# One hybrid decoder layer: splits four units ahead, the bias row's product inside the first unit, and operations moved between engines

## The reference

```
h = rmsnorm(x, pre_mix_norm);  rq, rk, rv, rg, mq, mk, mv = split(h @ w_in)
ret  = silu(rg) * head_rmsnorm(retention(rotary(rq), rotary(rk) / 8, rv))
moba = softmax(mq @ mk.T / 8 + bias_t[:, bucket(i - j)], causal) @ mv
x = x + rmsnorm(concat(ret, moba) @ w_out, post_mix_norm)
h = rmsnorm(x, pre_ffn_norm)
x = x + rmsnorm((silu(h @ w_gate) * (h @ w_up)) @ w_down, post_ffn_norm)
```

## Time and profile before

| | |
|---|---|
| median of 3 runs | 316.87 us (316.57 to 318.9) |
| the profiled execution's own time | 318.91 us |
| its span, first to last instruction | 317.1 us |
| TensorE busy | 305.3 us, 96% of the span |
| VectorE, ScalarE, GpSimd busy | 182.7, 153.3, 27.6 us |
| granted TensorE clock | 0.998 of full speed |

### The profile page before, as it was taken

How to read it: one execution, slowest core, us unless ns; L and a number is a source line. 1 busy time by engine, 2 the same in 40 slices (tenths; PEclk the granted TensorE clock), 3 DMA queues, 4 the chain that set the end, 5 groups by cost and what they waited for, 6 DMA issues and landing times.

```text
span 317.1 us, 4124 instructions
## 1 busy us (share of the span) xinstructions
PE 305.3 (96%) x1432; PEld 248.8 (78%) x1432; DVE 182.7 (58%) x255; ACT 153.3 (48%) x254; POOL 27.6 (9%) x31
## 2 busy tenths in 40 slices
PE   7999987999999999999999999999999999999992
PEld 3788866888888888768888888888888888888881
DVE  2858265697467487899555555544444454551426
ACT  4889626446608174676444444444433333340322
POOL 4021056000002000540000000000000000000001
PEclk9999999999999999999999999999999999999999
DMA  6999974314541543169965555555566565400003
GB/s 216 398 407 373 413 308 134 134 66 153 180 144 57 198 156 111 66 231 317 367 203 179 179 190 180 168 184 191 198 198 198 198 196 183 149 0 0 0 2 132
DMA packets 17517, 58.35 MB, mean 184 GB/s; under 512 B 1997, under 2 KB 2517, under 8 KB 17504
## 3 DMA queue, kind: packets, MB, share of 16 engines
q1 hardware_dynamic: 17136, 57.06, 51.6%
q0 software_dynamic: 368, 1.11, 1.0%
HBM read 57.10 MB, written 1.06 MB: 183 GB/s over the span
## 4 chain that ended last, share of the span: by engine, by line
PE 85%; DVE 7%; ACT 3%; DMA 2%; POOL 2%; issue 1%; SPq 0%; DVEq 0%
PE bank L951 25%; PE bank L953 24%; PE bank L952 24%; PE bank L961 4%; DVE w_lo L681 2%; DMA raw<-in_w_in 2%; PE bank L978 1%; POOL xs L437 1%; PE bank L982 1%; PE bank L986 1%; ACT w_hi L451 1%; DVE d_lo L876 1%; ACT kz L518 1%; PE bank L1049 1%; DVE res L942 1%
## 5 line engine op out<-in xcount | busy, mean ns | idle before, releaser
L951 PE MATMUL bank<-w_hi,a_hi 128*128 128x512 f32 x256 | 101.9, 398 | 0.0
L953 PE MATMUL bank<-w_hi,a_lo 128*128 128x512 f32 x256 | 100.1, 391 | 0.0
L952 PE MATMUL bank<-w_lo,a_hi 128*128 128x512 f32 x256 | 99.6, 389 | 0.0
L617 ACT ACTIVATE sil<-bank,rstd 128x256 f32<-128x256 f32 x22 | 10.4, 473 | 96.1 <-PE bank L953 93.7
L953 PEld LDWEIGHTS bank<-w_hi,a_lo 128*128 128x128 f32 x256 | 48.0, 188 | 10.6
L952 PEld LDWEIGHTS bank<-w_lo,a_hi 128*128 128x128 f32 x256 | 48.2, 188 | 9.8
L951 PEld LDWEIGHTS bank<-w_hi,a_hi 128*128 128x128 f32 x256 | 48.1, 188 | 9.4
L869 DVE TENSOR_TENSOR w_lo<-raw,w_hi 128x1024 fp32r<-128x1024 f32 x40 | 49.6, 1276 | 6.7 <-ACT w_hi L602 6.7
L681 DVE TENSOR_TENSOR w_lo<-raw,w_hi 128x1024 fp32r<-128x1024 f32 x32 | 42.2, 1345 | 19.4 <-ACT w_hi L451 19.4
L884 DVE SCALAR_TENSOR_TENSOR hid<-bank,rstd,sil 128x256 f32<-128x256 f32 x22 | 10.7, 485 | 73.9 <-ACT sil L617 73.9
L602 ACT ACTIVATE w_hi<-raw 128x1024 fp32r<-128x1024 f32 x40 | 40.5, 1057 | 0.5 <-DMA raw<-in_w_gu 0.5
(11 more groups left out here) (119 smaller groups left out, 307.5 us busy)
## 6 DMA issues: line engine op xcount, KB each, us to landing
raw<-in_w_gu SPq DMA_DIRECT2D x44, 512.0 KB, 4.3
raw<-in_w_dn SPq DMA_DIRECT2D x22, 512.0 KB, 4.6
raw<-in_w_in SPq DMA_DIRECT2D x20, 512.0 KB, 8.5
raw<-in_w_out SPq DMA_DIRECT2D x8, 512.0 KB, 3.2
raw<-in_w_in SPq DMA_DIRECT2D x8, 256.0 KB, 5.8
xs<-in_x SPq DMA_DIRECT2D x2, 512.0 KB, 8.6
bias<-bias_row POOLq DMA_DIRECT2D x1, 1024.0 KB, 10.2
out<-res SPq DMA_DIRECT2D x4, 256.0 KB, 2.0
```

The lines of the kernel that those rows point to most:

```text
L617: act.activation(sil[:, t, :], pg[:, t, 0:FG], ACT.Silu, scale=rstd[:, X1_, t:t + 1]).then_inc(sil_ready[t], 1)
L951: pe.matmul(acc, hi, wh, start=first, stop=False)
L952: pe.matmul(acc, hi, wl, start=False, stop=False)
L953: return pe.matmul(acc, lo, wh, start=False, stop=last)
```

## The change

- `LEAD` is 4: in slot u unit u + 4 is split. The order before the loop loses unit 4, which comes in slot 0.
- The bias row's product stands between the two halves of unit 0; its two tables are issued from ScalarE's queue, ahead of everything there.
- `gp` and `gm` are loaded behind units 8 and 9, not 16 and 18. VectorE, not GpSimd, makes `xg` in slots 7 and 8 and `gp = gm * gp` in slot 9, each behind its lo.
- The copies of k into `kz` are shared: ScalarE the even heads, VectorE the odd ones, at the head of its slot 10.
- `rows_out` for q, k and v stands ahead of hi in slots 4, 8 and 12.
- `xs += mix` stays on GpSimd for tile 0 and goes to VectorE for tile 1, behind lo_gu(1, 1 to 3).
- In the feed-forward part group 1 accumulates in `bank45` and group 0 is turned into `bank01`, so that gate_up(1, 0) need not wait for the first hidden tiles; these are turned in the middle of gate_up(1, 1). In every group both gate_up come first, then down(g - 1, 0), both turns, down(g - 1, 1); ScalarE's and VectorE's orders follow.

```diff
-LEAD = 5
-LO_UNITS = {16: [], 17: [21], 18: [22], 19: [23, 24]}
+LEAD = 4
+LO_UNITS = {16: [], 17: [20], 18: [21], 19: [22, 23]}
...
+G0 = 7
...
-        pg = bank01
-        pt = bank45
+
+        def pg(g):
+            return bank45 if isinstance(g, int) and g == 1 else bank01
+
+        def pt(g):
+            return bank01 if isinstance(g, int) and g == 0 else bank45
...
-                if n == 16:
+                if n == 8:
                     sp.dma_start(gp[:, :], g_pre_ffn.broadcast_to([P, D])).then_inc(gp_loaded, 16)
-                if n == 18:
+                if n == 9:
                     sp.dma_start(gm[:, :], g_post_mix.broadcast_to([P, D])).then_inc(gm_loaded, 16)
...
-            pool.dma_start(rel[0:BUCKETS, :], rel_bias).then_inc(rel_loaded, 16)
-            pool.dma_start(bucket[:, :], bucket_c).then_inc(rel_loaded, 16)
...
-            pool.wait_ge(gp_loaded, 16)
-            pool.wait_ge(gm_loaded, 16)
-            for t in range(NT):
-                pool.wait_ge(x_loaded[t], 16)
-                pool.tensor_tensor(xg[:, t, :], xs[:, t, :], gp[:, :], ALU.mult).then_inc(xg_ready, 1)
-            pool.wait_ge(xg_ready, NT)
-            pool.tensor_tensor(gp[:, :], gm[:, :], gp[:, :], ALU.mult).then_inc(xg_ready, 1)
             pool.wait_ge(k_turned, NT)
-            pool.wait_ge(xg_ready, NT + 1)
+            pool.wait_ge(rstd_ready, NT)
...
+            for c in range(2):
+                cols = slice(c * CW, (c + 1) * CW)
+                pool.wait_ge(mixn_ready, c + 1)
+                pool.tensor_tensor(xs[:, 0, cols], xs[:, 0, cols], mix[:, 0, cols], ALU.add
+                                   ).then_inc(x1_ready[0], 1)
             for t in range(NT):
-                for c in range(2):
-                    cols = slice(c * CW, (c + 1) * CW)
-                    pool.wait_ge(mixn_ready, 2 * t + c + 1)
-                    pool.tensor_tensor(xs[:, t, cols], xs[:, t, cols], mix[:, t, cols], ALU.add
-                                       ).then_inc(x1_ready, 1)
                 factor(FACTORS.index((X1_, t)))
...
+            act.dma_start(bucket[:, :], bucket_c).then_inc(rel_loaded, 16)
+            act.dma_start(rel[0:BUCKETS, :], rel_bias).then_inc(rel_loaded, 16)
...
-            hi_in(4)
...
                 if u == K_T + 1:
                     for t in range(NT):
                         act.wait_ge(k_turned, t + 1)
-                        for odd in range(2):
-                            rows = slice(64 * odd, 64 * odd + 64)
-                            act.activation(kz[rows, odd:MH:2, t * P:(t + 1) * P],
-                                           wk[rows, t, :].rearrange("p (b i) -> p b i", i=P), ACT.Copy
-                                           ).then_inc(kT_ready, 1)
+                        act.activation(kz[0:64, 0:MH:2, t * P:(t + 1) * P],
+                                       wk[0:64, t, :].rearrange("p (b i) -> p b i", i=P), ACT.Copy
+                                       ).then_inc(kT_ready, 1)
+                if u == UPG:
+                    act.wait_ge(nq_ready, 1)
+                    wait_factor(act, X_, NT - 1)
+                    rows_out(qn, 0, lambda t: nq[:, t:t + 1], q_nat)
+                if u == 2 * UPG:
+                    rows_out(kn, 1, r_x, k_nat)
+                if u == 3 * UPG:
+                    rows_out(v, 2, r_x, v_nat)
                 hi_in(u + LEAD)
...
             def group(g, g0, more=True):
 
+                if g0 > 1:
+                    h_hi_part(g - 1, 1)
                 if more:
                     for s in range(GU - 1):
                         hi_gu(g + 1, s, g0 + 1)
                 silu(g, 0)
-                h_hi_part(g - 1, 1)
+                if g0 == 1:
+                    for t in range(NT):
+                        h_hi_part(0, t)
                 if more:
                     hi_gu(g + 1, GU - 1, g0 + 1)
+                silu(g, 1)
                 for j in range(DN):
                     hi_dn(g, j, g0)
-                silu(g, 1)
                 h_hi_part(g, 0)
...
+            hi_gu(1, 3, 1)
             wait_factor(act, X1_, 0)
             silu(0, 0)
-            hi_gu(1, 3, 1)
             x1_squares(1)
-            hi_dn(0, 0, 0)
             wait_factor(act, X1_, 1)
             silu(0, 1)
-            h_hi_part(0, 0)
-            hi_dn(0, 1, 0)
+            for j in range(DN):
+                hi_dn(0, j, 0)
...
             for u in range(N_IN):
+                if u == K_T + 1:
+                    for t in range(NT):
+                        dve.wait_ge(k_turned, t + 1)
+                        dve.tensor_copy(kz[64:P, 1:MH:2, t * P:(t + 1) * P],
+                                        wk[64:P, t, :].rearrange("p (b i) -> p b i", i=P)
+                                        ).then_inc(kT_odd, 1)
...
+                if 0 <= u - G0 < NT:
+                    t = u - G0
+                    dve.wait_ge(gp_loaded, 16)
+                    dve.wait_ge(x_loaded[t], 16)
+                    dve.tensor_tensor(xg[:, t, :], xs[:, t, :], gp[:, :], ALU.mult).then_inc(xg_ready, 1)
+                if u == G0 + NT:
+                    dve.wait_ge(gm_loaded, 16)
+                    dve.wait_ge(xg_ready, NT)
+                    dve.tensor_tensor(gp[:, :], gm[:, :], gp[:, :], ALU.mult).then_inc(xg_ready, 1)
...
             def group(g, g0, more=True):
+                if g0 > 1:
+                    h_lo_part(g - 1, 1)
                 if more:
                     for s in range(GU - 1):
                         lo_gu(g + 1, s, g0 + 1)
                 hidden(g, 0)
-                h_lo_part(g - 1, 1)
+                if g0 == 1:
+                    for t in range(NT):
+                        h_lo_part(0, t)
                 if more:
                     lo_gu(g + 1, GU - 1, g0 + 1)
+                hidden(g, 1)
                 for j in range(DN):
                     lo_dn(g, j, g0)
-                hidden(g, 1)
                 h_lo_part(g, 0)
...
             factor(X1_, 0, 10)
-            lo_gu(1, 1, 1)
+            for s in range(1, GU):
+                lo_gu(1, s, 1)
+            dve.wait_ge(mixn_ready, 2 * NT)
+            for c in range(2):
+                cols = slice(c * CW, (c + 1) * CW)
+                dve.tensor_tensor(xs[:, 1, cols], xs[:, 1, cols], mix[:, 1, cols], ALU.add
+                                  ).then_inc(x1_ready[1], 1)
             hidden(0, 0)
-            lo_gu(1, 2, 1)
-            lo_gu(1, 3, 1)
             factor(X1_, 1, 12)
-            lo_dn(0, 0, 0)
             hidden(0, 1)
-            h_lo_part(0, 0)
-            lo_dn(0, 1, 0)
+            for j in range(DN):
+                lo_dn(0, j, 0)
             group(1, 1)
...
+            def bias_row_product():
+
+                pe.wait_ge(rel_one, 1)
+                pe.wait_ge(rel_loaded, 32)
+                pe.matmul(wk[0:MH, 0, 0:REV], rel[:, :], bucket[:, :], start=True, stop=True
+                          ).then_inc(brow_done, 1)
+
...
+                    if k == 0:
+                        bias_row_product()
...
-                if not (isinstance(g, int) and g == 0):
+                if not (isinstance(g, int) and g <= 1):
                     pe.wait_ge(hid_ready[t], g)
...
+            def first_hidden(s):
+                if s == 1:
+                    for t in range(NT):
+                        turn_hidden(0, t)
+
             def group(g, g0):
-                gate_up(g, 0, g0)
-                turn_hidden(g - 1, 1)
+                for t in range(NT):
+                    gate_up(g, t, g0, hook=first_hidden if g0 == 1 and t == 1 else None)
                 down(g - 1, 0, g0 - 1)
-                gate_up(g, 1, g0)
-                turn_hidden(g, 0)
+                for t in range(NT):
+                    turn_hidden(g, t)
                 down(g - 1, 1, g0 - 1)
...
             gate_up(0, 0, 0, hook=scaled_hook)
             gate_up(0, 1, 0)
-            turn_hidden(0, 0)
             group(1, 1)
             with pe.Fori(2, NF - 2, 2) as g:
                 group(g, 2)
                 group(g + 1, 3)
             group(NF - 1, NF - 1)
-            turn_hidden(NF - 1, 1)
             down(NF - 1, 0, NF - 1, last=True)
             down(NF - 1, 1, NF - 1, last=True)
```

More of the change, by code:

```diff
@@ L237, in hybrid_layer @@
         mixn_ready = sem("mixn_ready")
-        x1_ready = sem("x1_ready")
+        x1_ready = [sem(f"x1_ready{t}") for t in range(NT)]
         gu_done = sem("gu_done")
@@ L529, in _ @@
                         squares(X_, u, c, xs[:, u, c * CW:(c + 1) * CW])
-                if u == UPG:
-                    act.wait_ge(nq_ready, 1)
-                    wait_factor(act, X_, NT - 1)
-                    rows_out(qn, 0, lambda t: nq[:, t:t + 1], q_nat)
-                if u == 2 * UPG:
-                    rows_out(kn, 1, r_x, k_nat)
-                if u == 3 * UPG:
-                    rows_out(v, 2, r_x, v_nat)
                 if u == RQK_T + 1:
@@ L883, in hidden @@
```

(17 more changed lines are left out.)

15 lines of the change are left out of this document (5 added, 10 removed).

## The result

The changed kernel takes 318.91 us (median of 20 executions, 316.61 to 320.86), the kernel before 316.86 us (20 executions, 316.11 to 321.17). The ratio is 1.0046 (95% interval 1.0025 to 1.0066): **slower by 0.5%**, where 314.5 us was forecast. It lies above the range (317.0).

The account below looks back on a forecast made before the run. TensorE, busy 96% of the span, was taken as the bound. Start and input phase 2.8 less feed-forward 0.4 gave 2.4 us, so 314.5 us against the median 316.87; range 311.5 to 317.0, own range 313.3 to 315.9.

Parts of the forecast that it names:

- its own time, then how it stands to the median: Final sum: 2.4 us off the profiled 318.91 gives 316.5; against the median of three runs, 316.87, it gives 314.5.
- the ends of part 3: Start and input phase gain: 4.0 us if copies are in time, about 1 if unit 12 lands 1.8 later.
- part 3: Input phase: lock waits of 1.6 and 2.2 us go; unit 12 lands about 32.2, new 0.85 us wait before head 0.
- part 5: First feed-forward groups: 1.2 us wait goes, down(0, 0) waits 2.1 us; a loss of 0.4 us in all.
- Why the scores wait: Input phase: GpSimd's operation locks VectorE out, so two lo take 3.17 and 3.23 us instead of 1.22.
- The rule on memsets: Shared port: GpSimd's memsets do not lock VectorE and cost nothing; if they did, the sum would give 315.5.
- Part 1, the start: Bias row's product moved into a 1.43 us TensorE stall: gain 0.45 us, bounds a gain of 0.7 and loss of 0.5.
- Part 2: LEAD 4: only reorders, squares of x come one hi earlier in slots 0 to 2; costs nothing.
- the gain is taken back in front of head 0: Rival: unit 12 lands 1.8 us later still, or VectorE's copies queue behind it; about 316.2 us, chance 0.2.
- Part 4, the ring: Head 0 to head 3: chain of logits, exponentials, hi, lo and v takes 10.8 us, from 39.5 to about 50.4.
- Part 6: Feed-forward loop and end: same products and turns in another order, worth nothing if hidden(g, 1) is ready in time.
- the loop rival: Rival: hidden(g, 1) 0.85 us late in each loop period, ten times, 8.5 us slower, 323 us; chance 0.08.

Follow-up runs that it names:

- the last experiment: Kernel before with only xg and gp = gm * gp moved to VectorE's slots 20 and 22, loads left where they were: 315.40 us, ratio 0.9932.
- the kernel with the old start: Late products and loads, early hidden splits, but bias row product after unit 1 and tables from GpSimd's queue; against the kernel before: 313.67 us, ratio 0.9875.

## Why the prediction was wrong

**The account that the runs give.** From the usual before (316.9): no lock -1.6, start -0.9, feed-forward order -0.8, together 313.6; measured, without the early loads and products, 313.72. So the lead, the shared k copies, `rows_out` ahead of hi and the moved adds come to about nothing together; the last two were never run alone. On top come the early loads, +1.3, and, as the remainder, the products in slots 7 to 9, +2.0: 317.0, which is what the changed kernel takes in the six executions with the highest clocks. In two executions of three the clock falls and it takes about 2 more: median 319.

**The error of 4.4 us in its parts**, by the start of the scores of head 3: the profiled before 53.24, forecast 50.4, the usual before 51.40, after 51.89. The base is 1.8 of it (53.24 - 51.40), the longer wait before head 0 is 1.5 (51.89 - 50.4), the clock about 2.0 (318.91 less the 316.88 of the profile; 1.6 of it is the fall as profiled, the rest is the scatter whose cause is open), and the feed-forward part gives back 1.2 (0.8 gained where a loss of 0.4 was forecast). That makes 4.1; 0.3 is left, no more than single profiles beside medians leave.

**The base.** Step "its own time, then how it stands to the median". The profiled execution of before was the rare kind, with both lo caught; I took its 3.8 us of waits as the usual ones and then subtracted the gain from the median, which has only 1.6. The spread of the three times shown, 316.57 to 318.9, was the hint, and I read it as noise. My own range had a slip too: from the ends of part 3 and the 0.4 of part 5 its upper end is 316.3, not 315.9; it left out the measured time either way. Against the profiled execution the sum gave 316.5 us with a span of 314.7; the profile of after has 316.88 and 315.0. That agreement is luck: two errors with opposite signs, the longer wait before head 0 and the better feed-forward part, in an execution that kept its clock.

**Why the scores wait.** Right in its mechanism: nothing but the three products was moved in the last experiment and the 3.2 us of a lo became 1.22. The rule on memsets (the Trainium skill, page "SBUF — State Buffer", section "SBUF: two separate sides") held too: GpSimd's two memsets run from 36.20 to 37.30, VectorE's xg begins at 36.37 and takes 1.22 like any other.

**Part 1, the start.** The row was misread. I took `a_hi` at 11.86 for block 4 and let it bound the gain. It is block 5; block 4 was ready earlier (after the change it starts at 10.83, and TensorE goes on at 12.22 with no idle time), so nothing bounded the gain. In the kernel with the old start the next product comes at 13.03, in the best version at 12.10, though 0.12 us before this place the old start was ahead (11.52 against 11.64): the product costs 1.05 us there, the 0.74 from 12.29 to 13.03 and 0.3 ahead of it, and 0.9 was measured in all against the forecast 0.45. In the changed kernel it buys nothing, as I had said, because head 0 waits for VectorE.

**Part 2.** Right for its own cost: nothing, in the version with late loads. But it is the lead, not the earlier product, that brings the load of `bias` forward (25.42 and 21.97 above), on which part 3 counts; whether a lead of 5 would have helped beside the early loads was not run.

**Part 3, the term that failed.** The mechanism was right: a wait before head 0 on the copies of `kz` from VectorE, set off by the landing of unit 12. Its size was 2.83 and 3.42 us, not 0.85. Unit 12 landed 1.5 us later than summed (33.7, not 32.2), and the copies were done at 41.19, not 39.5. With loads and bias together I had added 4.2 us. Measured, the kernel with late loads has unit 12 at 28.8 against 28.0, so `bias` adds at most about 0.8 where I had 1.7, and the early loads a further 4.9 in the changed kernel (33.7) and 5.6 in the one without its early products (34.4), for which 2.5 had been worked out from bytes over bandwidth. A later landing also leaves more of the bias load in front, but that is by my own rate another 0.8 us or so (0.3 MB). With it, 3.3 is accounted for, and 3.3 is what units 13 and 14 were late by; the further 2.3 of unit 12 fell on it alone. It landed 1.5 us before unit 13 and not 3.8, as if the two had moved side by side; why is open. The written order did as summed: from the landing to the end of the copies 7.5 us were measured (33.7 to 41.19) and 7.3 summed; hi(12) began 0.3 after the landing and lo(12) 0.2 after hi(12), since VectorE was still at the first xg, begun at 34.10.

**Not foreseen: the clock.** A wait three to four times as long as forecast is also one after which TensorE can lose half its clock, for 3.4 us in the profile that shows it (after 3.42 us of idle time; after 2.83 it kept its clock). The profile of before has waits of at most 2.20 us in this phase and no fall. The rival "the gain is taken back in front of head 0" (0.2, 316.2 us) had the place and the reason right, with unit 12 later still, but neither the clock nor the base.

**Part 4, the ring.** Right: from head 0 to head 3 I had 39.5 to 50.4, 10.9 us; it took 10.6, with the wait before head 3 gone to 0.20 since head 0 was late. TensorE alone is nearly as slow: with late products and loads it goes from head 0 to head 3 in the same 10.6, without a wait.

**Part 5.** Nearly right on the wait before down(0, 0), 2.1 us forecast and 1.73 measured. Against the old order the first groups come out some 0.2 ahead (down(0, 1) at 145.92 against 145.85, with a turn of 0.23 less to come), where I had a loss of 0.4. **Part 6** gave some 0.5 where I had nothing; the loop rival (323 us) did not happen in any way.

**What the best version is.** The changed kernel with the loads and products late and the first hidden splits early: 312.78 us, 1.5% under before and 1.9% under the changed kernel.

## What to carry to other kernels

Work that an engine does for a later stage belongs in a slot in which nobody waits for that engine and the transfers are not full: an engine's low busy share there can mean, as here, that it waits for a landing, and what is written ahead of its chain comes on top of that landing. A small load put ahead of a unit in a full queue can put that unit off by twice its bytes over the bandwidth, as unit 12 here (5.6 us for 2.5), and the units behind it by less (3.3). And before a gain is subtracted, find out which of several kinds of execution the profile shows: a wait that hangs on the phase of two engines is there in some and not in others.

## What was not expected of the hardware

- An idle time of TensorE of 3.42 us between two full stretches was followed, 1.4 us after work resumed, by 3.4 us at 1.2 GHz; the execution with 2.83 us kept 2.4 GHz. 22 of 32 executions of this kernel have the lower mean clock; the fall costs 1.6 us between the two profiles. With 2.4 us or more of filler products in the same wait (10 or 20 of them) none of 24 has.
- Two broadcasts of 512 KB, moved ahead of a unit in a full queue, put its landing off by 5.6 us and that of the next two units by 3.3; 1.05 MB at the some 410 GB/s of the windows in which they were issued is 2.5.
- A float32 product of ident with itself, 128 x 128, took 0.23 us (20 in 4.6), as long as a product of 128 x 512 in the rounded parts.
